# Slab splits, first tiles and norm roots regrouped at the boundaries between projections of a transformer stack

## What is computed

```python
# first block, two layers; norm = rmsnorm
for i in range(2):
    hn = norm(h, g[0])
    m = rwkv_pool_mixer(hn, ...) if i == 0 else diff_attn_mixer(hn, ...)   # each ends in @ w_out
    h = h + norm(m, g[1])
    h = h + norm(square(relu(norm(h, g[2]) @ w1)) @ w2, g[3])
# second block, one layer
u = norm(x) @ w_in
y = concat(ssd_mixer(u_ssd), mla_mixer(u_mla)); x = x + y @ w_out
x = x + memory_attention(norm(x), norm(mem), wq, wk, wv, wo)       # 256 memory rows, 4 heads of 256
x = x + (silu(g) * val) @ w_down,  where g, val = split(causal_conv(norm(x) @ w_up))   # 5632 wide
out = norm(x)
```

## Time and profile before

| | |
|---|---|
| three timed runs | 2478.63, 2486.38 (median), 2487.91 us |
| the profiled execution, its own time | 2496.84 us |
| its span, first to last instruction | 2495.0 us |
| mean granted TensorE clock | 0.963 |
| busy in the span | PE 94%, DVE 57%, ACT 43%, POOL 20% |
| slab splits in it | ACT L438 328.1 us, DVE L460 407.9 us, 186 each |

### The profile page before, as it was taken

One profiled execution on the slowest core, in us unless ns is written; L12 is line 12 of the kernel. 1 busy time (PEld: TensorE's weight loads), 2 busy tenths in 40 slices (PEclk: granted clock), 3 DMA queues, 4 the chain that ended last, 5 costly groups with the idle time before them and its releaser, 6 DMA issues. The chain is left out here.

```text
span 2495.0 us, 41785 instructions
## 1 busy us (share of the span) xinstructions
PE 2340.3 (94%) x16659; PEld 1680.9 (67%) x16669; DVE 1417.0 (57%) x2230; ACT 1067.4 (43%) x1855; POOL 495.2 (20%) x530
## 2 busy tenths in 40 slices
PE   7999879999999999899999999988889988899998
PEld 5889768888877776774445865656647877644445
DVE  6575566533266765566532576664636345687733
ACT  6435443322245556432223355366644454333322
POOL 0276440002223541510012302044330000000000
PEclk9998899999999998989999999998989999999999
DMA  4211012222111112013222212011022230232222
GB/s 164 86 36 36 35 68 102 102 102 98 64 63 52 52 60 68 35 71 115 102 107 88 96 68 102 18 60 43 1 68 95 109 136 1 94 109 102 81 95 79
DMA packets 38938, 190.96 MB, mean 77 GB/s; under 512 B 12176, under 2 KB 14608, under 8 KB 17624
## 3 DMA queue, kind: packets, MB, share of 16 engines
q1 hardware_dynamic: 37944, 186.08, 21.1%
q10 hardware_dynamic: 800, 2.20, 0.3%
HBM read 185.08 MB, written 3.19 MB: 75 GB/s over the span
## 5 line engine op out<-in xcount | busy, mean ns | idle before, releaser
L460 DVE SCALAR_TENSOR_TENSOR wsp<-raw_w,wsp 128x2048 f16<-128x2048 f32 (+2 forms) x186 | 407.9, 2193 | 175.6 <-ACT wsp L438 170.0
L419 PE MATMUL ps<-hn,wsp 128*128 128x512 f16 x1968 | 430.9, 380 | 6.9 <-DVEq L242 4.8
L438 ACT ACTIVATE wsp<-raw_w 128x2048 f16<-128x2048 f32 (+2 forms) x186 | 328.1, 1764 | 117.6 <-PE ps L417 48.2
L414 PE MATMUL ps<-hn,wsp 128*128 128x256 f16 (+1 forms) x2592 | 313.7, 285 | 41.0 <-DVEq L242 15.9
L419 PEld LDWEIGHTS ps<-hn,wsp 128*128 128x128 f16 x1968 | 192.1, 98 | 235.2 <-DVEq L242 5.3
L419 PE MATMUL ps<-big,wsp 128*128 128x512 f16 (+1 forms) x1740 | 344.1, 359 | 4.7 <-DVEq L242 4.7
L417 PE MATMUL ps<-hn,wsp 128*128 128x264 f16 x2880 | 337.0, 280 | 3.6 <-DVE hn L721 3.6
L414 PEld LDWEIGHTS ps<-hn,wsp 128*128 128x128 f16 x2592 | 261.1, 102 | 89.7 <-POOL hn L894 19.4
L417 PEld LDWEIGHTS ps<-hn,wsp 128*128 128x128 f16 x2880 | 283.8, 99 | 53.1 <-issue 4.9
L419 PEld LDWEIGHTS ps<-big,wsp 128*128 128x128 f16 x1740 | 171.5, 99 | 166.9 <-issue 8.1
L414 PE MATMUL ps<-big,wsp 128*128 128x256 f16 (+1 forms) x2184 | 248.0, 275 | 9.3 <-DVE big L3100 4.5
(11 more groups left out here) (428 smaller groups left out, 3018.3 us busy)
## 6 DMA issues: line engine op xcount, KB each, us to landing
raw_w<-slabs SPq DMA_DIRECT2D x162, 1024.0 KB, 5.2
raw_w<-slabs SPq DMA_DIRECT2D x10, 512.0 KB, 4.0
raw_w<-slabs SPq DMA_DIRECT2D x8, 384.0 KB, 5.1
h<-xin SPq DMA_DIRECT2D x2, 1056.0 KB, 7.2
out<-hn SPq DMA_DIRECT2D x8, 256.0 KB, 2.1
big<-memx ACTq DMA_DIRECT2D x1, 1024.0 KB, 4.8
sml<-small SPq DMA_DIRECT2D x1, 768.0 KB, 14.4
cst<-consts SPq DMA_DIRECT2D x1, 582.0 KB, 13.2
```

Of the source, the lines that this page charges most:

```text
L414: mm = L.eng.matmul(ps[:rows, b, 0:T // 2], lhsT, rhs[:, z, :], start=first, stop=last)
L419: mm = L.eng.matmul(two(ps[:rows, b, 0:T]), lhsT, rhs, start=first, stop=last)
L438: L.fin(L.eng.activation(wsp[:, n % NW, 0, lo:hi], raw_w[:, q % 2, at:at + hi - lo], ACT.Copy, scale=WSCALE), "hi")
L460: ins = L.eng.scalar_tensor_tensor(wsp[:, n % NW, 1, lo:hi], raw_w[:, q % 2, at:at + hi - lo], WSCALE, wsp[:, n % NW, 0, lo:hi], ALU.mult, ...
```

## The change

- In `gemm_grid` the first two tiles of a head grid are one group; the spread of the post heads comes after 24 units in place of 18.
- Slab splits at tails go by halves: the high halves after the passes of m = 3 and of m = 4, the low halves likewise. At heads: one high half, root(s), the other high half, then the first evacuation; on DVE in the post heads one low half, the reciprocals, the other.
- `post_add` makes three additions of half a tile width of tokens, one for each square and one for the cross product, each waiting for its own operand, in place of one addition of both squares and one of the cross product.
- Layer 0's w_out: scales, high and low parts of the group norm are placed earlier, the pooled halves at m = 3 and 5.
- MLA attention: `pair_dve` one unit later, the pieces of the up slab one unit earlier from the third on.
- The second block's w_out waits for 15 operands and takes the sixteenth at its last k.
- Memory attention: the last slab split ahead of ACT's copies goes in four pieces into units 66 to 69 (low parts 67 to 70).

```diff
@@ layout
-        UP_HI, UP_LO = {19: 2, 20: 2, 22: 2, 23: 2, 24: 1}, {20: 2, 21: 2, 23: 2, 24: 2, 25: 1}
+        UP_HI, UP_LO = {19: 2, 20: 2, 21: 2, 22: 2, 23: 1}, {20: 2, 21: 2, 22: 2, 23: 2, 24: 1}
@@ gemm_grid
-            gated = 3 if halved and not head else 2 if src and not halved else 1
+            gated = 3 if halved and not head else 2 if src else 1
...
-                            norm_step_pe(L, cnt, T, 1, head, done[z])
+                            norm_step_pe(L, cnt, T, 1, head, done[z], 24)
@@ post_add
-            L.take("post_sq", 2)
-            add(rs_acc2[:, :, cols], sq[:, :, cols], "sq_added")
-            L.tell("sq_added")
+            for acc in (rs, acc2):
+                q = cnt["post_sq"] = cnt.get("post_sq", -1) + 1
+                L.take("post_sq")
+                add(acc, sq[:, q % 2, cols], "sq_added")
             u = cnt["cross"] = cnt.get("cross", -1) + 1
             L.take("cross")
-            add(acc3[:, cols], cross[:, u % 2, cols], "cross_added")
+            add(acc3, cross[:, u % 2, cols], "cross_added")
@@ PE, second block
-            L.take("mix2", 16)
-            gemm_deep(L, cnt, 16, 16, 2, lambda k: zt(k), SEQ, tail="late", mid=mem_norm)
+            L.take("mix2", 15)
+            gemm_deep(L, cnt, 16, 16, 2, lambda k: zt(k), SEQ, src=lambda k: L.take("mix2", k == 15), tail="late",
+                      mid=mem_norm)
@@ grid_tail_act (the memory part's tail likewise)
-                if m == 3:
-                    split_hi(L, cnt)
                 for j in ((), (0,), (1, 2), (3,), (4,), (5,), (6, 7), ())[m]:
                     pass_act(L, T, 0, j, dst, y)
+                if m in (3, 4):
+                    split_hi_part(L, cnt)
@@ mlp_act (second_act likewise; the late heads with late_root_act)
-            split_hi(L, cnt)
+            split_hi_part(L, cnt)
             post_roots_act(L, T, 1)
+            post_root2_act(L, T, 1)
+            split_hi_part(L, cnt)
             relu_half(0, 0)
-            post_root2_act(L, T, 1)
@@ memory attention, ACT
-                if m % 4 == 3:
+                if m % 4 == 3 and m < 23:
                     split_hi(L, cnt)
...
+                if 66 <= n < 70:
+                    split_hi_part(L, cnt, 2)
@@ layer 0's w_out, ACT
+                if m in (4, 6):
+                    gn_high(1, 3 * (m - 4) // 2)
                 post_evac(L, cnt, T0, mo, lambda j: V("norm_g", 8 + j), m, 0)
...
-                if m >= 4:
-                    gn_high(1, m - 4)
+                if m in (4, 5):
+                    gn_high(1, m - 3)
@@ grid_tail_dve
-                    if j == 4:
-                        split_lo(L, dcnt)
+                if m in (3, 4):
+                    split_lo_part(L, dcnt)
@@ attention, DVE
-                if i == 3 and hd % 2 == 0 and hd:
+                if i == 0 and hd % 2 and hd > 1:
                     pair_dve(hd // 2 - 1)
@@ memory attention, DVE
-            for n in range(6):
+            for n in range(5):
                 split_lo(L, dcnt)
...
+                if 67 <= n < 71:
+                    split_lo_part(L, dcnt, 2)
@@ FFN up, DVE
-                if m % 4 == 3:
+                if m in (2, 3):
+                    split_lo_part(L, dcnt)
+                elif m % 4 == 3:
                     split_lo(L, dcnt)
@@ layer 0's w_out, DVE
-                if 3 <= m < 7:
-                    gn_scale(1, m - 3)
-                if m >= 4:
-                    gn_low(1, m - 4)
+                for j in {3: (0, 1), 4: (2,), 5: (3,)}.get(m, ()):
+                    gn_scale(1, j)
+                for j in {4: (0,), 5: (1,), 6: (2, 3)}.get(m, ()):
+                    gn_low(1, j)
```

More of the change, by code:

```diff
@@ L322, in build @@
         acc3 = late(T0)
-        rs_acc2 = wk[:, 2 * T0:8 * T0].rearrange("p (a t) -> p a t", a=2)
         cross = late(2, T0)
@@ L553, in gemm_grid, with norm_step_pe @@
                         between(m)
-        def norm_step_pe(L, cnt, T, z, kind, done):
+        def norm_step_pe(L, cnt, T, z, kind, done, spread=18):
             if done == (12 if kind == "post" else 8):
                 norm_sums_pe(L, cnt, T, z, kind)
-            if done == (18 if kind == "post" else 13):
+            if done == (spread if kind == "post" else 13):
                 norm_spread_pe(L, cnt, T, z, kind)
@@ L573, in gemm_deep @@
                         for k in range(kk):
-                            if first and j == 0 and src:
+                            if first and j == 0 and callable(src):
+                                src(k0 + k)
+                            elif first and j == 0 and src:
                                 L.take(src)
@@ L2005, in second_act @@
             flat = lambda t: t.rearrange("p a b -> p (a b)")
-            split_hi(L, cnt)
+            split_hi_part(L, cnt)
             post_roots_act(L, SEQ, 1)
+            post_root2_act(L, SEQ, 1)
+            split_hi_part(L, cnt)
             x_unit(0, 0)
-            post_root2_act(L, SEQ, 1)
             for m in range(1, 8):
@@ L2203, in q_unit @@
                         split_hi(L, cnt)
-            split_hi(L, cnt)
+            split_hi_part(L, cnt)
+            late_root_act(L, SEQ)
+            split_hi_part(L, cnt)
             q_unit(0, 0)
-            late_root_act(L, SEQ)
             for m in range(1, 8):
@@ L2913, in second_dve @@
                     pass_dve(L, SEQ, 0, j, h2, n2, gain)
-                if m == 4:
-                    split_lo(L, dcnt)
+                if m in (3, 4):
+                    split_lo_part(L, dcnt)
             root_inverse_dve(L, SEQ)
@@ L3374, in grid_tail_pool @@
                 for m in range(8):
-                    if at2 and m in (3, 4):
+                    if at2 and m in (3, 5):
                         at2(m)
```

13 lines of the change are left out of this document (7 added, 6 removed).

## The result

The changed kernel takes 2470.01 us (median of six runs, 2461.71 to 2477.57) against 2487.14 of the kernel before in the same session (six runs, 2478.63 to 2490.72): a ratio of 0.9937, 95% interval 0.9912 to 0.9963, that is 9 to 22 us less. The forecast was 2462.6 with a range of 2444 to 2480, a saving of 23.8 us. The time lies in the range; the saving, 17.1 us between the medians, is smaller than forecast, and the 23.8 lie a little outside the interval.

What follows compares the result with a forecast made beforehand. TensorE was taken to bound the kernel (busy 2340.3 of 2495.0 us), leaving waits at projection boundaries and half clock to win. Nine terms summed to 23.8 us off the median 2486.38, giving 2462.6, range 2444 to 2480.

Steps and rivals of the forecast that it cites:

- signs named for a wrong forecast: PE's summed waits for evacuations growing at the heads, or half-clock stretches staying with the waits gone.
- Layer 0's w_out: Second half: of PE's 4.34 us wait for the group norm's low pass, 3.3 go.
- Post-norm heads: Two mlp ups 0.6 us each, second w_in 0.5, layer 1's qkv 0.3: 2.0 saved, POOL's chain setting the end.
- Second w_in: Its head, one of the post-norm heads, was to save 0.5 us.
- Memory q head: PE's whole 3.43 us wait for the spread factors goes, the root coming after one high half: 3.4 saved.
- FFN up: At its head the pair begins 2.7 us later, but the spread isn't waited for: 0.5 us saved.
- Attention: Slab for the up projection 2.1 us, pairs' step one unit later 2.0, end of attention 4.4 saved.
- Memory attention: The 4.22 us wait at its start goes, four units grow by 2.9 in all: net 1.3 us saved.
- Clock: Half-clock stretches at layer 0's w_out, 1718.9 and attention's end: 9.6 us at full clock, half taken, 4.8.
- The pair's gate: Rival, chance 0.06: at the heads the second bank comes too late and the pair's start decides; slower, 2508.0 us.
- The clock gives all of it: Rival, chance 0.12: the 9.6 us come whole and three heads keep full clock, 4.1 each; 2445.5 us.
- the ends stay pinned: Rival, chance 0.18: POOL, ACT and DVE still set the ends, clock unchanged; only 10.5 us saved, 2475.9 us.

Runs made afterwards that it cites:

- d4: Changed kernel with the last slab split whole ahead of the memory attention's copies again; ratio 0.9922 to the kernel before.
- e3: Kernel before with only the three half-width POOL additions of `post_add`; ratio 1.0000 to the kernel before, median 2481.7 us.
- d3: Changed kernel with DVE's reciprocals first and then both low halves at the post heads, as before; ratio 0.9939 to the kernel before.
- d2: Changed kernel with POOL's two additions a tile (whole and half) in place of three halves; 2468.7 us, ratio 0.9926 to the kernel before.
- e1: Changed kernel with low halves behind the reciprocals and pairs of first tiles only at the two mlp ups; 2461.5 us, ratio 0.9911 to the kernel before.
- e2: e1 with whole additions in w_out's first half only and eight smaller memory attention pieces; 2457.2 us, ratio 0.9886 to the kernel before.
- d1: Changed kernel with single first tiles at the head grids and the spread after 18 units again; ratio 0.9906 to the kernel before.
- b2: Kernel before with the change's boundary parts alone (pairs of first tiles, halved splits, roots, additions, group norm); ratio 0.9961 to the kernel before.
- b1: Kernel before with the attention parts of the change alone (pair step, up slab, sixteenth operand, memory attention pieces); ratio 0.9940 to the kernel before.

## Why the prediction was right, and where it was not

The way and the range were right; the sum was higher than the timed saving (23.8 against 16 to 18). By stretches of the traces it seems to fit (22 to 27 us behind the scan, by which profiles are taken), but in part by luck: terms that were too high and a gain that was not counted cancel, as the list shows. What is left of the difference is not explained; the clock of single launches moves by as much, and two profiles of a kernel don't average it.

Of the signs named for a wrong forecast, one came: PE's waits for evacuations grew, from 4.8 to 21.4 us. It did not make the change a loss, for of the 31.6 us waited for the slab and for POOL's low halves all but 2.3 went with it. PE's idle time, forecast near 135 us, was 140.0 and 145.4. The other sign, half clock that stays with the waits gone, came at one of three places (see the clock below).

- **Layer 0's w_out.** About right in size with its mlp up (3.9 to 6.0 us of 4.9 by the four pairs of profiles, 2.4 to 3.7 by d4). The step "the operand is there at about 301.5" held, but what is late next was POOL, filled by three additions a tile, which I had not named there.
- **Post-norm heads.** The pair's later start (3 us reckoned, 3.6 measured) and the end set by POOL's chain came out as said. The step that failed is the price of the additions, "the three separate additions ... take about as long": it counts POOL's own time and not that a whole addition holds DVE (1.53 us instead of 0.46). In the profiles they alone are worth 5.0 us at layer 1's mlp up (e3), 2.7 up to the sums and 2.3 behind them. The term was 0.6.
- **Second w_in.** Forecast 0.5 gained, 1 to 2 lost. The failing step: I put the first low half ahead of the reciprocals at no cost, though POOL paced PE there (PE waited 2.88 us for one of its low halves in the kernel before) and the trace of before showed POOL slowed by DVE's splits. It costs 2.1 us of wait (d3), and the three additions have a part in it (3.34 us of wait with two in d2, 5.26 with three); up to 2 more are clock, which e1 and e2 show to go either way.
- **Memory q head.** 3.4 forecast, 3.6 measured against the first profile of before and 3.1 against the second, the same in every profile of the changed kernel.
- **FFN up.** 0.5 gained forecast, 0.4 to 1.0 lost. PE stood 7.75 us for the pair where it had stood 4.49 for the single tile, more than the freed spread gave back: without the pair the stretch is 2.3 to 2.8 shorter (d1). In b2 the pair stood as long, but the clock came back sooner and the stretch took 368.1, so the loss is not there in every launch.
- **Attention.** The slab wait fell from 2.94 to 0.62, by 2.3 where 2.1 were forecast. Pairs, end and their clock: 9.1 forecast, 6.2 to 8.8 measured.
- **Memory attention.** 4.2 ahead and 2.9 back forecast; 3.5 to 4.2 and 2.2 to 4.2 measured. Net 1 to 2, and about nothing where the clock fell in the units.
- **Clock.** 4.8 taken for the waits removed. This term was too high. PE in the same three places of the changed kernel, layer 0's w_out, the up slab and the end of attention:

```profile
296.40:303.30 6.90, 6.90 (x39) 0.51 0.01 2
1702.70:1706.20 3.50, 3.50 (x10) 0.51 1.02 421
1811.90:1818.80 6.90, 4.89 (x17) 0.51 0.00 0
```

The busy time at half clock is 15.3 us there (13.8 in the second profile) instead of 19.3, and half of the difference, 2.0 to 2.8 us, is won. In w_out it grew, from 4.25 to 6.90, behind the new wait for POOL. Another piece lies where I had counted none, at layer 1's mlp up. The rule of the Trainium skill that the rivals name (TensorE: Matmul & The Clock Gate, Terms) would make of 23.9 throttled us there before and some 10.2 in e3 an estimate of 6.8 us. All that the stretch gained is 5.0, of which 2.3 behind the sums, so where PE stands the rule gives too much.
- **The rivals.** *The pair's gate* never came to decide at the post heads: POOL was later by 0.95 and 1.87 us at layer 1's. At the late head it did decide, at the small price above. *The clock gives all of it* (2445.5) fell, since the three places gave 2.0 to 2.8 us of 9.6, and *the ends stay pinned* (2475.9) is missed by 5.9 us and the forecast by 7.4, so the time alone speaks for neither; the pairs and the end of the attention and the clock behind them gave 6.2 to 8.8 us, which that case had left out.

## What to carry to other kernels

Ask of a chain that paces a boundary how each instruction slows its neighbour on another engine, in its form too, before its length: at layer 1's mlp up three short additions beat two longer ones by 0.9 us a round, though their own time was longer, because a whole one held the other engine. Moving work forward is free only if nothing that is waited for runs beside it. And the busy work behind a wait may run at half speed or not with the same waits (e1 and e2 differ by 2.0 us at the second w_in), so cost a gap with the stretch that follows it, and don't trust such a gain from one profile.

## What was not expected of the hardware

- The same program's launches spread over up to 20 us (2463.8 to 2484.0 in twelve of b1) with mean granted clocks of 0.974 to 0.966, the longer ones at the lower clock, while most waits repeat to 0.15 us.
- DVE's two-input addition of 128x256 took 1.53 us when a GpSimd addition of 128x512 had begun just before it, ending 0.28 us behind it, and 0.46 beside additions of 128x256; GpSimd's three additions took 4.40 us beside DVE's slab split and 2.33 without it.
